# Decoder block pair on one core: stick-breaking q and k, gates and gated projections computed feature-major

## The chip, the cores and the metric

One core of one Trainium2 chip. The metric is the device time of one launch in microseconds, the median of several executions. Everything is float32 outside; the large products run in three matmuls of a rounded float32 type (fp32r), as told below.

## The reference, cut to what matters

Two transformer layers in a row over 256 tokens with 2048 features. The change lies in the second one, whose core is:

```python
proj = h @ w_in
c_q, c_kv, k_pe, q_sb, k_sb, v_sb, gl_a, gl_b = jnp.split(proj, [...], axis=-1)
...
y_a = _mla_attention(...)            # 8 heads
# stick-breaking attention, 8 heads of 128, on q_sb, k_sb, v_sb
z = einsum('bhqd,bhkd->bhqk', qb, k) * 128 ** -0.5
log_beta = log_sigmoid(z)
log_one_minus = where(mask, log_sigmoid(-z), 0.0)
tail = cumsum(log_one_minus, axis=3, reverse=True) - log_one_minus
a = where(mask, exp(log_beta + tail), 0.0)
y_b = einsum('bhqk,bhkd->bhqd', a, v)
...
merged = sigmoid(gl_a) * (y_a @ w_proj_mla) + sigmoid(gl_b) * (y_b @ w_proj_sb)
x = x + gt1 * (merged @ w_out)
```

q_sb, k_sb and v_sb have 1024 features each, gl_a and gl_b 2048 each.

## The kernel before, in words

**Chunks.** All weights are read once, in chunks of 256 input features by 512 output features (512 KB). SP fetches each into `raw`, a ring of four (`sp_chunk`, L301). ScalarE rounds it to `hi` (`act_chunk`, L309), VectorE forms the rest `lo = raw - hi` (`dve_chunk`, L315), and TensorE multiplies (`pe_chunk`, L317 to L333). The operand (activations) is also held in two parts, `op_hi` and `op_lo`, with features in the partitions and 256 tokens in the columns. In `pe_chunk` the operand is the stationary side (128 features x 128 tokens, loaded as weights) and the chunk's 512 output features stream past it; for two token tiles and two feature tiles of the contraction there are three matmuls each: hi with hi (L328), lo with hi (L329), hi with lo (L330), 12 in all. The result has tokens in the partitions. It collects in one of two pairs of PSUM banks (`acc`), and an eviction frees the pair. `chunk_used` counts chunks that TensorE has finished, `lo_ready` those that it may take; ScalarE may round into a ring place when the chunk four earlier is used.

**The order of the second layer** is written out by hand over a chunk number G, the same on each engine (`sp_second`, `act_second`, `dve_second`, `pe_second`). Each engine walks G and does its part of chunk G, then the side steps hung on that G. The stages that the change touches, in order: G 17 to 24 first half of stick q; then latent up-projections; `in2b`, 40 chunks: second half of q, k (two blocks), v (two blocks), eight chunks a block; `in2c`, 64 chunks: the eight gate blocks, sigmoid at the eviction; `pp`, 32 chunks: y_a and y_b times their projections, four chunks a block; `out2`, 32 chunks. ENDS gives the chunk at which block n of the 36 is complete; its eviction is hung on the third G after that (`act_read2`, L1847 to L1849).

**Stick attention** runs beside the gates in four groups of two heads, 16 chunks a group (`stick_at`). Within a group, at the step given (an engine's own step: ScalarE and VectorE run up to three chunks ahead of TensorE): 2 ScalarE copies q, k, v of two heads from `proj` to `s_in` (L1927); 3 TensorE transposes q and k, eight 128x128 blocks (L2284); 6 ScalarE and VectorE copy them to `s_qk`, q scaled (L1930, L2097); 5 TensorE scores (L2295, L2296); 8 ScalarE and VectorE log-sigmoids, TensorE the tail sums; 11 and 12 exponential and mask, TensorE times v (L1836 to L1838); 14 the eviction to `y_b`.

**Gated projections.** VectorE multiplies each finished pp block into its gate (L2195) and adds the two halves (L2199), counted in `gated`. The sum is in `proj` with tokens in the partitions; to be the operand of the output projection it must have features in the partitions. `pe_merged` transposes it (L2318, four 128x128 blocks per pair of feature tiles, eight pairs), ScalarE evicts to `stage` (L494), and VectorE rounds to `op_hi` (L508) and subtracts to `op_lo` (L509), counted in `op_ready`.

**Other lines named:** L1131 matmuls of 128 columns in the first layer's recurrence; L2326 to L2328 the key product (`pe_key_product`, G 16): there the weights, 64 columns wide, are the stationary side, and op_hi and op_lo with 256 tokens stream past, 16 contraction tiles by three matmuls into one place.

Of the kernel before, what the change touches and what calls it, by code (L numbers as in the profile page):

```python
# [24 lines left out]
P = 128  # L25
# [80 lines left out]
def build_program(nc, a, out):  # L106
    V, A, T = nc.vector, nc.scalar, nc.tensor
    with ExitStack() as ctx:
# [101 lines left out]
        with ExitStack() as use:  # L210
# [10 lines left out]
            with ExitStack() as inner:  # L221
                s_in = sb("s_in", [P, TT, 3, GW], stack=inner)
                s_qk = sb("s_qk", [P, GH_HEADS, 2 * S], stack=inner)
                s_l = sb("s_l", [P, GH_HEADS, TRI], stack=inner)
                s_n = sb("s_n", [P, GH_HEADS, TRI], stack=inner)
# [66 lines left out]
        for name, n in (("h1", 8), ("rec", 4), ("ffn1", 8), ("h2", 8), ("merged", 8), ("ffn2", 8)):  # L292
            OG[name] = g
            g += n
# [1074 lines left out]
        def sp_gu(sp, n, w):  # L1369
# [4 lines left out]
            def pair(i, with_ada):  # L1374
                for c, (m, k) in enumerate(pair_order(i)):
                    sp_chunk(sp, CH[f"gu{n}"] + c, i, 16, src(i, m, k))
                    if with_ada:
                        if n == 2 and not later(i) and c == 3:
                            sp.wait_ge(op_ready, OG["merged"] + 8)
                        ada_at(i, c)  # L1380
# [364 lines left out]

        def in2_src(G):
# [68 lines left out]
        sk = {n: sem("stick_" + n) for n in ("in", "tr", "q", "k", "z", "l", "n", "b", "tail", "w", "e", "a", "o", "op")}  # L1815
# [6 lines left out]
        gated = sem("gated")  # L1822
# [24 lines left out]
        def act_read2(act, n, dst, func):  # L1847
            done2(act, n)
            A.activation(dst, acc[:, bank2(n)], func).then_inc(acc_free[bank2(n)], 1)  # L1849
# [68 lines left out]
        def act_stick(act, g, at):  # L1918
            if at == 2:
                if g == 0:  # L1920
                    act.wait_ge(ml["o"], GROUPS)
                    act.wait_ge(acc_free[bank2(15)], freed2(15))
                else:
                    act.wait_ge(sk["o"], g)
                src = proj[:, :, SB0:FREE0].rearrange("p t (d n) -> p t d n", d=3)[:, :, :, g * GW:(g + 1) * GW]
# [19 lines left out]
        def act_second(act):  # L1945
            h2 = lambda g: act_operand(act, OG["h2"], 8, lambda m: mod[:, m:m + 1], lambda m: ada[:, m:m + 1], only=[g])
            merged = lambda g: act_operand(act, OG["merged"], 8, None, only=[g])
            for G in range(G_END):
# [5 lines left out]
                if n is not None:  # L1954
# [8 lines left out]
                    elif n == 3:  # L1963
                        act_read2(act, n, proj[:, :, SB0:SB0 + NB], ACT.Copy)
# [4 lines left out]
                    elif n < 16:  # L1969
                        act_read2(act, n, proj[:, :, SB0 + (n - 10) * NB:SB0 + (n - 9) * NB], ACT.Copy)  # L1970
                    elif n < 24:
                        act_read2(act, n, gate_cols(n - 16), ACT.Sigmoid)
# [23 lines left out]
                for g in range(GROUPS):  # L1996
                    if 2 <= G - mla_at(g) <= 8:
                        act_mla(act, g, G - mla_at(g))
                    if 2 <= G - stick_at(g) <= 14:
# [94 lines left out]
        def dve_stick(dve, cd, g, at):  # L2094
            if at == 6:
                dve.wait_ge(sk["q"], g + 1)
                V.tensor_copy(s_qk[:, :, S:2 * S], tp[:, :, S:2 * S]).then_inc(sk["k"], 1)  # L2097
# [15 lines left out]
        def dve_second(dve, cd, out_readout):  # L2113
            merged = lambda g: dve_operand(dve, cd, OG["merged"], 8, 0, only=[g])
            after = dve_second_steps(dve, "in2", xw2)
            for G in range(G_END):
# [57 lines left out]
                for g in range(GROUPS):  # L2174
                    if 3 <= G - mla_at(g) <= 10:
                        dve_mla(dve, cd, g, G - mla_at(g))
                    if 6 <= G - stick_at(g) <= 12:
# [96 lines left out]
        def pe_stick(pe, g, at):  # L2274
            if at == 3:
                pe.wait_ge(sk["in"], g * 2 + 2)
                if g:
                    pe.wait_ge(sk["w"], g)
                else:
                    pe.wait_ge(ml["pt"], GROUPS)  # L2280
                for h in range(GH_HEADS):
                    for j in range(2):
                        for t in range(TT):
                            ins = T.transpose(tp[:, h, (2 * j + t) * P:(2 * j + t + 1) * P], s_in[:, t, j, h * P:(h + 1) * P], ident)  # L2284
                ins.then_inc(sk["tr"], 1)
            if at == 5:
                pe.wait_ge(sk["q"], g + 1)
                pe.wait_ge(sk["k"], g + 1)
# [4 lines left out]
                for h in range(GH_HEADS):  # L2293
                    q, kk = s_qk[:, h, 0:S], s_qk[:, h, S:2 * S]
# [9 lines left out]
            if at == 11:  # L2304
                pe.wait_ge(sk["a"], g + 1)
                for h in range(GH_HEADS):
                    ins = causal_product(aux[:, h], [s_in[:, t, 2, h * P:(h + 1) * P] for t in range(TT)], s_b[:, h])
                ins.then_inc(sk["o"], 1)

        def pe_merged(pe, g):  # L2310
            j = g // 2
            pe.wait_ge(gated, j + 1)
            Gm = OG["merged"] + g
            pe.wait_ge(stage_ready, CK * (Gm - 1))
            for kk in range(CK):
                for t in range(TT):
                    col = (CK * (g % 2) + kk) * P
                    ins = T.transpose(tp[:, Gm % 2, kk * S + t * P:kk * S + (t + 1) * P], gate_cols(j)[:, t, col:col + P], ident)  # L2318
            ins.then_inc(tp_ready, 1)
# [11 lines left out]
        def pe_second(pe, h2):  # L2331
            n = 0
            for G in range(G_END):
# [5 lines left out]
                if G == 16:  # L2339
                    pe_key_product(pe, c, B2 + n)  # L2340
                elif G < G_UP:
                    k = G % 8 if G < 16 else G - 17
# [30 lines left out]
                for g in range(GROUPS):  # L2373
                    if 0 <= G - mla_at(g) <= 7:
                        pe_mla(pe, g, G - mla_at(g))
                    if 3 <= G - stick_at(g) <= 11:
# [3 lines left out]
                for j in (0, 1):  # L2380
                    if G - (G_PP + 9 + 8 * j) in (0, 1):
                        pe_merged(pe, 2 * j + G - (G_PP + 9 + 8 * j))
                if G in (G_OUT - 2, G_OUT - 1):
                    pe_merged(pe, 4 + G - (G_OUT - 2))
                if G in (G_OUT + 1, G_OUT + 2):
                    pe_merged(pe, 6 + G - (G_OUT + 1))
# [156 lines left out]
```

## Time and profile before

| what | value |
|---|---|
| median of 3 runs | 2608.74 us (2608.72 to 2609.54) |
| span of the profiled execution, first to last instruction | 2606.9 us |
| what lies around the span, by the median | 1.8 us |
| instructions | 33516 |
| TensorE matmuls, busy | 11881, 2587.1 us |
| weight loads, busy | 11881, 2145.5 us |
| VectorE, ScalarE busy | 1825.4 us, 1414.8 us |
| read from memory | 578.55 MB, 223 GB/s over the span |

The profiled execution's own total isn't reported apart from its span, so the median stands for it. PE is TensorE's matmuls, PEld its weight loads, DVE VectorE, ACT ScalarE. Rows of matmuls overlap: each row runs from its issue to the modelled end of its drain, so the pace is read from the distances of the starts, not from the durations. A product of plain float32 shows as two matmuls.

### The profile page before, as it was taken

To read this page: it belongs to the slowest core of one execution; us is meant where nothing else is said; L and a number is where in the kernel's file an instruction comes from. 1 tells how busy PE (TensorE), PEld (TensorE's weight loads), DVE (VectorE), ACT (ScalarE), POOL (GpSimd) and SP (SyncE) were. 2 spreads that over 40 slices of the span, in tenths; PEclk is the share of its full clock that TensorE was granted. 3 is DMA by queue.
4 is the path that set the end of the run, shared out by engine and by line. 5 is a ranking of instruction groups with operands and counts; after the bars stand their busy time and mean duration, and the time that the engine had idled before them with its cause. 6 is when DMAs were issued, how large, how long until landed. Compare 5 with 4: busy or idle time off the path is not lost.

```text
span 2606.9 us, 33516 instructions
## 1 busy us (share of the span) xinstructions
PE 2587.1 (99%) x11881; PEld 2145.5 (82%) x11881; DVE 1825.4 (70%) x2168; ACT 1414.8 (54%) x1861; POOL 14.6 (1%) x28
## 2 busy tenths in 40 slices
PE   9999999999999999999999999999999999999999
PEld 7888888878888888888788888888788888888887
DVE  5888888777777878888875545566687654445565
ACT  6555545465656465445566556544465556565443
POOL 1000000000000000000000000000000000000000
PEclk9999999999999999999999999999999999999999
DMA  7765556778888888887665555555578765655554
GB/s 247 253 194 178 170 151 205 268 262 291 283 292 285 291 285 297 283 293 253 199 202 157 167 171 160 184 204 186 183 269 289 254 198 191 195 190 197 192 193 172
DMA packets 302590, 582.20 MB, mean 223 GB/s; under 512 B 20133, under 2 KB 20913, under 8 KB 302097
## 3 DMA queue, kind: packets, MB, share of 16 engines
q1 hardware_dynamic: 301008, 576.26, 66.7%
q0 software_dynamic: 1008, 3.55, 0.4%
q8 instruction: 70, 1.15, 0.2%
q10 hardware_dynamic: 464, 0.93, 0.1%
q14 instruction: 40, 0.32, 0.0%
HBM read 578.55 MB, written 2.11 MB: 223 GB/s over the span
## 4 chain that ended last, share of the span: by engine, by line
PE 95%; DVE 3%; ACT 1%; issue 1%; DMA 0%; ACTq 0%; DVEq 0%
PE acc L328 30%; PE acc L330 30%; PE acc L329 30%; DVE lo L315 1%; PE aux L1131 1%; DVE op_lo L509 0%; PE tp L482 0%; DVE op_hi L508 0%; ACT stage L494 0%; PE tp L1105 0%; PE aux L2258 0%; PE aux L2257 0%; PE tp L542 0%; DMA rows<-attn_norm_w 0%; PE tp L1151 0%
## 5 line engine op out<-in xcount | busy, mean ns | idle before, releaser
L315 DVE TENSOR_TENSOR lo<-raw,hi 128x1024 fp32r<-128x1024 f32 x895 | 1077.2, 1222 | 430.5 <-ACT hi L309 409.6
L309 ACT ACTIVATE hi<-raw 128x1024 fp32r<-128x1024 f32 x895 | 928.3, 1056 | 528.5 <-PE acc L330 368.8
L328 PE MATMUL acc<-hi,op_hi 128*128 128x512 f32 x2752 | 1084.9, 394 | 8.5 <-DVE lo L315 5.9
L330 PE MATMUL acc<-hi,op_lo 128*128 128x512 f32 x2752 | 1072.1, 390 | 0.0
L329 PE MATMUL acc<-lo,op_hi 128*128 128x512 f32 x2752 | 1071.5, 389 | 0.0
L328 PEld LDWEIGHTS acc<-hi,op_hi 128*128 128x128 f32 x2752 | 516.9, 188 | 119.6 <-issue 11.2
L330 PEld LDWEIGHTS acc<-hi,op_lo 128*128 128x128 f32 x2752 | 516.6, 188 | 109.0
L329 PEld LDWEIGHTS acc<-lo,op_hi 128*128 128x128 f32 x2752 | 517.2, 188 | 102.6
L591 DVE SCALAR_TENSOR_TENSOR ada_acc<-ada_ring,cact,ada_acc 128x512 f32<-128x512 f32 x360 | 269.5, 749 | 7.6 <-DVE small L431 0.6
L328 PE MATMUL acc<-hi,f_hi 128*128 128x512 f32 x704 | 274.5, 390 | 0.1
L329 PE MATMUL acc<-lo,f_hi 128*128 128x512 f32 x704 | 273.9, 389 | 0.0
L330 PE MATMUL acc<-hi,f_lo 128*128 128x512 f32 x704 | 273.9, 389 | 0.0
L1408 ACT ACTIVATE hid<-f_g 32x256 f32 (+1 forms) x352 | 146.3, 416 | 66.7 <-DVE f_g L1473 58.7
L1575 ACT ACTIVATE f_hi<-hid 128x512 fp32r<-128x512 f32 x88 | 55.6, 632 | 227.4 <-PE acc L330 227.4
L328 PEld LDWEIGHTS acc<-hi,f_hi 128*128 128x128 f32 x704 | 132.2, 188 | 27.8 <-issue 0.5
L330 PEld LDWEIGHTS acc<-hi,f_lo 128*128 128x128 f32 x704 | 132.2, 188 | 27.4
L329 PEld LDWEIGHTS acc<-lo,f_hi 128*128 128x128 f32 x704 | 132.2, 188 | 27.2
L1595 DVE TENSOR_TENSOR f_lo<-hid,f_hi 128x512 fp32r<-128x512 f32 x88 | 60.8, 691 | 95.3 <-ACT f_hi L1575 94.7
L735 ACT ACTIVATE proj<-acc,small 128x512 f32<-128x512 f32 x32 | 20.3, 685 | 56.0 <-PE acc L330 54.8
L508 DVE CAST op_hi<-stage 128x512 fp32r<-128x512 f32 x41 | 17.4, 425 | 42.4 <-ACT stage L494 42.2
L1849 ACT ACTIVATE proj<-acc 128x1024 f32<-128x1024 f32 x23 | 23.6, 1027 | 22.8 <-PE acc L330 22.6
L1131 PEld LDWEIGHTS aux<-h_qd,h_kd 128*128 128x128 f32 x256 | 33.5, 191 | 2.5
(336 smaller groups left out, 1284.0 us busy)
## 6 DMA issues: line engine op xcount, KB each, us to landing
raw<-w_in SPq DMA_DIRECT2D x257, 512.0 KB, 3.9
ada_ring<-w_ada SPq DMA_DIRECT2D x192, 512.0 KB, 5.3
raw<-w_gate_up SPq DMA_DIRECT2D x176, 512.0 KB, 5.2
raw<-w_ffn_in SPq DMA_DIRECT2D x176, 512.0 KB, 4.4
raw<-w_down SPq DMA_DIRECT2D x88, 512.0 KB, 5.8
raw<-w_ffn_out SPq DMA_DIRECT2D x88, 512.0 KB, 4.3
raw<-w_out SPq DMA_DIRECT2D x64, 512.0 KB, 4.1
raw<-w_proj_mla SPq DMA_DIRECT2D x16, 512.0 KB, 3.9
```

What stands on the lines that cost most here:

```text
L309: A.activation(hi[:, k, :, 0:n], raw[:, k, :, 0:n], ACT.Copy).then_inc(hi_ready, 1)
L315: V.tensor_tensor(lo[:, k, :, 0:n], raw[:, k, :, 0:n], hi[:, k, :, 0:n].bitcast(F32), ALU.subtract).then_inc(lo_ready, 1)
L328: T.matmul(dst, lh, hi[:, k, kk, 0:n], start=first and kk == 0, stop=False)
L329: T.matmul(dst, lh, lo[:, k, kk, 0:n], start=False, stop=False)
L330: mm = T.matmul(dst, ll, hi[:, k, kk, 0:n], start=False, stop=last and kk == CK - 1)
L591: ins = V.scalar_tensor_tensor(out=ada_acc[:], in0=ring[:, j, kk], scalar=cact[:, m:m + 1], in1=ada_acc[:], op0=ALU.mult, op1=ALU.add)
L735: ins = A.activation(proj[:, t, dst0:dst0 + NB], src[:, t], func, scale=r0[:, t:t + 1])
L1131: ins = T.matmul(aux[:, s % 2, x4 * P:(x4 + 1) * P], kd[:, x4 * P:(x4 + 1) * P], qd[:, y4 * P:(y4 + 1) * P], start=True, stop=True)
L1408: A.activation(dst, src, ACT.Copy).then_inc(f["ev"], 1)
L1575: A.activation(f_hi[:, j % 2], hid[:, 2 * kc:2 * kc + 2, :], ACT.Copy).then_inc(f["sp"], 1)
L1595: V.tensor_tensor(f_lo[:, j % 2], hid[:, 2 * kc:2 * kc + 2, :], f_hi[:, j % 2].bitcast(F32), ALU.subtract).then_inc(lo_done, 1)
L1849: A.activation(dst, acc[:, bank2(n)], func).then_inc(acc_free[bank2(n)], 1)
```

## The change

Stick q, stick k, the gates and the projections of y_a and y_b are computed with the weights as the stationary side (`pe_turned`): for each of four feature tiles of 128 and two contraction tiles, 128x128 of `hi` or `lo` are loaded and 256 tokens of op_hi or op_lo stream past, three matmuls each, 24 a chunk. The result has features in the partitions. The four feature tiles of a block lie in the pair of banks as (bank f // 2, half f % 2). Stick v, the latents, the up-projections and the output projection stay as they were. `s_in`, `s_qk`, the transposes of q and k, `pe_merged` and its stages are gone; v is read from `proj` directly; q's scale is applied when its block is evicted; the merged sum is copied by ScalarE from `proj` to `op_hi`, and VectorE subtracts.

```diff
+        def pe_turned(pe, c, into, kt, first, last, right=(op_hi, op_lo)):
+            k = c % RING
+            pe.wait_ge(lo_ready, c + 1)
+            for f in range(NB // P):
+                for kk in range(CK):
+                    rh, rl = (o[:, kt + kk] for o in right)
+                    dst = into[:, f // 2, f % 2 * S:(f % 2 + 1) * S]
+                    wh, wl = (r[:, k, kk, f * P:(f + 1) * P] for r in (hi, lo))
+                    T.matmul(dst, wh, rh, start=first and kk == 0 and f % 2 == 0, stop=False)
+                    T.matmul(dst, wh, rl, start=False, stop=False)
+                    mm = T.matmul(dst, wl, rh, start=False, stop=last and kk == CK - 1 and f % 2 == 1)
+            mm.then_inc(chunk_used, 1)
...
+        def turned_head(which, head):
+            c0 = SB0 + which * DH + head // 4 * NB + head % 2 * S
+            return proj[:, head % 4 // 2, c0:c0 + S]
+
+        def merged_pair(g):
+            return gate_cols(g // 2)[:, g % 2]
...
+        def act_merged(act, g):
+            act.wait_ge(gated, g // 2 + 1)
+            if g >= 4:
+                act.wait_ge(chunk_used, C2 + G_OUT - 7 + g)
+            A.activation(op_hi[:, CK * g:CK * g + CK].rearrange("p k s -> p (k s)"), merged_pair(g), ACT.Copy).then_inc(merged_hi, 1)
...
         def act_stick(act, g, at):
-            if at == 2:
...
-                for t in range(TT):
-                    A.activation(s_in[:, t], src[:, t], ACT.Copy).then_inc(sk["in"], 1)
-            if at == 6:
-                act.wait_ge(sk["tr"], g + 1)
-                A.activation(s_qk[:, :, 0:S], tp[:, :, 0:S], ACT.Copy, scale=float(P) ** -0.5).then_inc(sk["q"], 1)
...
                     elif n < 24:
+                        if n == 23:
+                            act.wait_ge(sk["o"], GROUPS)
                         act_read2(act, n, gate_cols(n - 16), ACT.Sigmoid)
...
+            def merged(g):
+                dve.wait_ge(merged_hi, g + 1)
+                h, l = (o[:, CK * g:CK * g + CK].rearrange("p k s -> p (k s)") for o in (op_hi, op_lo))
+                V.tensor_tensor(l, merged_pair(g), h.bitcast(F32), ALU.subtract).then_inc(merged_ready, 1)
...
         def pe_stick(pe, g, at):
-            if at == 3:
...
-                            ins = T.transpose(tp[:, h, (2 * j + t) * P:(2 * j + t + 1) * P], s_in[:, t, j, h * P:(h + 1) * P], ident)
...
                 for h in range(GH_HEADS):
-                    q, kk = s_qk[:, h, 0:S], s_qk[:, h, S:2 * S]
+                    q, kk = (turned_head(j, GH_HEADS * g + h) for j in range(2))
...
             if at == 8:
                 pe.wait_ge(sk["n"], g + 1)
+                if g:
+                    pe.wait_ge(sk["w"], g)
+                else:
+                    pe.wait_ge(ml["pt"], GROUPS)
...
-                    ins = causal_product(aux[:, h], [s_in[:, t, 2, h * P:(h + 1) * P] for t in range(TT)], s_b[:, h])
+                    c0 = SB0 + 2 * DH + (GH_HEADS * g + h) * P
+                    ins = causal_product(aux[:, h], [proj[:, t, c0:c0 + P] for t in range(TT)], s_b[:, h])
...
-        def pe_merged(pe, g):
...
@@ pe_second
+                elif 16 < G < G_UP:
+                    pe_turned(pe, c, into, CK * (G - 17), G == 17, G == G_UP - 1)
...
-                    pe_chunk(pe, c, 0, 4, into, CK * k, k == 0, k == 7)
+                    if G_SB + 24 <= G < G_GATE:
+                        pe_chunk(pe, c, 0, 4, into, CK * k, k == 0, k == 7)
+                    else:
+                        pe_turned(pe, c, into, CK * k, k == 0, k == 7)
...
-                        pe_chunk(pe, c, 0, 4, into, CK * (k % 2), k == 0, k == 3, left=(ya_hi[k // 2], ya_lo[k // 2]))
+                        pe_turned(pe, c, into, CK * (k % 2), k == 0, k == 3, right=(ya_hi[k // 2], ya_lo[k // 2]))
...
-                        pe_chunk(pe, c, 0, 4, into, HEADS + CK * k, k == 0, k == 3)
+                        pe_turned(pe, c, into, HEADS + CK * k, k == 0, k == 3)
...
-                        pe.wait_ge(op_ready, OG["merged"] + k + 1)
+                        pe.wait_ge(merged_ready, k + 1)
```

## Rows read from the trace of the kernel before

**Rows 1.** The page: span, busy time by engine, TensorE's granted clock by slice.
```profile
span 2606.9 us, 33516 instructions
...
PE 2587.1 (99%) x11881; PEld 2145.5 (82%) x11881; DVE 1825.4 (70%) x2168; ACT 1414.8 (54%) x1861; POOL 14.6 (1%) x28
...
PEclk9999999999999999999999999999999999999999
```

**Rows 2.** The page: the chain that ended last, by engine.
```profile
PE 95%; DVE 3%; ACT 1%; issue 1%; DMA 0%; ACTq 0%; DVEq 0%
```

**Rows 3.** Waits of TensorE, 1299 to 1800 us: total us, times, longest.
```profile
PE acc L328 <- DVE lo L315: 0.4, 1, 0.4
```

**Rows 4.** Windows: length, busy PE, PEld, DVE, ACT, POOL (counts), clock, DMA, GB/s.
```profile
1298.92:1320.50 21.58, 21.58 (x104) 17.54 (x103) 20.86 (x27) 11.31 (x21) 0.00 (x0) 1.00 0.60 195
1361.10:1441.60 80.50, 80.14 (x404) 67.66 (x403) 45.78 (x57) 50.38 (x96) 0.00 (x0) 1.00 0.54 169
1496.30:1692.20 195.90, 195.90 (x948) 164.92 (x947) 99.01 (x90) 119.67 (x122) 0.00 (x0) 1.00 0.56 172
1692.20:1782.20 90.00, 90.00 (x411) 74.38 (x409) 59.65 (x62) 37.72 (x43) 1.07 (x2) 1.00 0.57 199
```

**Rows 5.** Timeline of PE (start us, us): 12 matmuls of 512, then 48 of 256.
```profile
1289.91 0.39 PE L328 MATMUL acc<-hi,op_hi 128*128 128x512 f32 x1
...
1292.40 0.39 PE L330 MATMUL acc<-hi,op_lo 128*128 128x512 f32 x1
1292.63 0.28 PE L2326 MATMUL acc<-op_hi,hi 128*64 128x256 f32 x1
...
1297.96 0.28 PE L2328 MATMUL acc<-op_lo,hi 128*64 128x256 f32 x1
```

**Rows 6.** Timeline of PEld around a block of eight 128-wide matmuls, first layer.
```profile
121.23 0.86 PEld L1131 LDWEIGHTS aux<-h_qd,h_kd 128*128 128x128 f32 x7
122.01 0.19 PEld L328 LDWEIGHTS acc<-hi,op_hi 128*128 128x128 f32 x1
122.12 0.19 PEld L329 LDWEIGHTS acc<-lo,op_hi 128*128 128x128 f32 x1
```

**Rows 7.** Timeline of PE around the first block of eight stick transposes.
```profile
1507.06 0.39 PE L330 MATMUL acc<-hi,op_lo 128*128 128x512 f32 x1
1507.29 1.03 PE L2284 MATMUL tp<-plain,s_in 128*128 128x128 f32 x8
...
1508.40 0.40 PE L329 MATMUL acc<-lo,op_hi 128*128 128x512 f32 x1
```

**Rows 8.** Timeline of PE around the first block of four merged transposes.
```profile
1719.31 0.39 PE L330 MATMUL acc<-hi,ya_lo 128*128 128x512 f32 x1
1719.54 0.60 PE L2318 MATMUL tp<-plain,proj 128*128 128x128 f32 x4
...
1720.21 0.39 PE L329 MATMUL acc<-lo,ya_hi 128*128 128x512 f32 x1
```

**Rows 9.** Groups by line, 1490 to 1805 us: count, busy us, mean ns, idle before.
```profile
L494 ACT ACTIVATE stage<-tp 128x256 f32<-128x256 f32 x16 | 5.3, 382 | 16.8 <-PE tp L2318 16.8
L2318 PE MATMUL tp<-plain,proj 128*128 128x128 f32 x32 | 4.8, 272 | 0.0
L2284 PE MATMUL tp<-plain,s_in 128*128 128x128 f32 x32 | 4.1, 272 | 0.0
L508 DVE CAST op_hi<-stage 128x512 fp32r<-128x512 f32 x8 | 3.4, 425 | 7.3 <-ACT stage L494 7.3
```

**Rows 10.** Timeline of PE: score products in plain float32, 256 and 128 wide.
```profile
1513.62 0.59 PE L2295 MATMUL aux<-s_qk 128*128 128x256 f32 x2
...
1514.05 0.38 PE L2296 MATMUL aux<-s_qk 128*128 128x128 f32 x2
...
1514.27 0.60 PE L2295 MATMUL aux<-s_qk 128*128 128x256 f32 x2
```

**Rows 11.** Timeline of DVE at the start of the output projection.
```profile
1783.38 1.22 DVE L2199 TENSOR_TENSOR proj<-proj 128x1024 f32<-128x1024 f32 x1
```

More of the change, by code:

```diff
@@ L291, in build_program @@
         g = 0
-        for name, n in (("h1", 8), ("rec", 4), ("ffn1", 8), ("h2", 8), ("merged", 8), ("ffn2", 8)):
+        for name, n in (("h1", 8), ("rec", 4), ("ffn1", 8), ("h2", 8), ("ffn2", 8)):
             OG[name] = g
@@ L1378, in pair @@
                         if n == 2 and not later(i) and c == 3:
-                            sp.wait_ge(op_ready, OG["merged"] + 8)
+                            sp.wait_ge(merged_ready, 8)
                         ada_at(i, c)
@@ L1812, in done2 @@
             eng.wait_ge(chunk_used, C2 + END_OF[n] + 1)
-        sk = {n: sem("stick_" + n) for n in ("in", "tr", "q", "k", "z", "l", "n", "b", "tail", "w", "e", "a", "o", "op")}
+        sk = {n: sem("stick_" + n) for n in ("z", "l", "n", "b", "tail", "w", "e", "a", "o", "op")}
         lt = {n: sem("latent_" + n) for n in ("sq", "var", "root", "ready", "tr", "ev", "split")}
@@ L1821, in build_program @@
         s_ang = sem("angles")
-        gated = sem("gated")
+        gated, merged_hi, merged_ready = sem("gated"), sem("merged_high"), sem("merged_ready")
         added, tail = sem("added"), sem("last_scaled")
@@ L1844, in latent, with act_read2 @@
             return proj[:, :, j * S:(j + 1) * S]
-        def act_read2(act, n, dst, func):
+        def act_read2(act, n, dst, func, scale=1.0):
             done2(act, n)
-            A.activation(dst, acc[:, bank2(n)], func).then_inc(acc_free[bank2(n)], 1)
+            A.activation(dst, acc[:, bank2(n)], func, scale=scale).then_inc(acc_free[bank2(n)], 1)
+        def act_merged(act, g):
[3 more added lines that the diff above has]
+            A.activation(op_hi[:, CK * g:CK * g + CK].rearrange("p k s -> p (k s)"), merged_pair(g), ACT.Copy).then_inc(merged_hi, 1)
         def act_latent_squares(act, l):
@@ L1946, in act_second @@
             h2 = lambda g: act_operand(act, OG["h2"], 8, lambda m: mod[:, m:m + 1], lambda m: ada[:, m:m + 1], only=[g])
-            merged = lambda g: act_operand(act, OG["merged"], 8, None, only=[g])
+            merged = lambda g: act_merged(act, g)
             for G in range(G_END):
@@ L1963, in act_second @@
                     elif n == 3:
-                        act_read2(act, n, proj[:, :, SB0:SB0 + NB], ACT.Copy)
+                        act_read2(act, n, proj[:, :, SB0:SB0 + NB], ACT.Copy, float(P) ** -0.5)
                     elif n < 11:
@@ L1969, in act_second @@
                     elif n < 16:
-                        act_read2(act, n, proj[:, :, SB0 + (n - 10) * NB:SB0 + (n - 9) * NB], ACT.Copy)
+                        act_read2(act, n, proj[:, :, SB0 + (n - 10) * NB:SB0 + (n - 9) * NB], ACT.Copy,
+                                  float(P) ** -0.5 if n == 11 else 1.0)
                     elif n < 24:
+                        if n == 23:
+                            act.wait_ge(sk["o"], GROUPS)
                         act_read2(act, n, gate_cols(n - 16), ACT.Sigmoid)
@@ L2274, in pe_stick @@
         def pe_stick(pe, g, at):
-            if at == 3:
[L2276 to L2283, printed above, removed]
-                            ins = T.transpose(tp[:, h, (2 * j + t) * P:(2 * j + t + 1) * P], s_in[:, t, j, h * P:(h + 1) * P], ident)
-                ins.then_inc(sk["tr"], 1)
             if at == 5:
-                pe.wait_ge(sk["q"], g + 1)
-                pe.wait_ge(sk["k"], g + 1)
+                if g == 0:
+                    for n in (14, 15):
+                        pe.wait_ge(acc_free[bank2(n)], freed2(n))
                 if g:
@@ L2306, in pe_stick @@
                 for h in range(GH_HEADS):
-                    ins = causal_product(aux[:, h], [s_in[:, t, 2, h * P:(h + 1) * P] for t in range(TT)], s_b[:, h])
+                    c0 = SB0 + 2 * DH + (GH_HEADS * g + h) * P
+                    ins = causal_product(aux[:, h], [proj[:, t, c0:c0 + P] for t in range(TT)], s_b[:, h])
                 ins.then_inc(sk["o"], 1)
-        def pe_merged(pe, g):
[L2311 to L2319, printed above, removed]
         def pe_key_product(pe, c, b):
@@ L2340, in pe_second @@
                     pe_key_product(pe, c, B2 + n)
+                elif 16 < G < G_UP:
+                    pe_turned(pe, c, into, CK * (G - 17), G == 17, G == G_UP - 1)
                 elif G < G_UP:
-                    k = G % 8 if G < 16 else G - 17
+                    k = G % 8
                     pe_chunk(pe, c, 0, 4, into, CK * k, k == 0, k == 7, late=OG["h2"] + 1 if G == 0 else None)
```

25 lines of the change are left out of this document (3 added, 22 removed).

## Prediction, made before the changed kernel ran

> **What bounds the kernel now.** I read the page first. TensorE is busy for 2587.1 of 2606.9 us at a granted clock of nine tenths or more in every slice, so at the upper of its two levels, 2.4 GHz [rows 1]. The chain that ended last is 95% TensorE [rows 2]. The reader should not conclude from a busy engine alone that it is the bound, since matmul rows overlap; so I asked what TensorE waited for over the stretch that the change touches: one wait of 0.4 us in 501 us [rows 3]. The windows, cut at the edges of the four touched stages (first half of stick q; second half and k; gates; gated projections), say the same: TensorE fills them, at clock 1.00, but for 0.36 us in the second [rows 4]. VectorE and ScalarE have slack in all but the first (VectorE 20.86 of 21.58 us in the q block), and there TensorE still doesn't wait. Hence the price of any edit is the time it adds to or takes from the row of matmul starts, and what it does on the other engines costs nothing while they keep ahead.
>
> **Base of the sum.** The profiled execution spans 2606.9 us; the runs have a median of 2608.7 (2608.7 to 2609.5). What lies around the span is 1.8 us, which I add back at the end.
>
> **What is taken off TensorE.** Transposes of stick q and k: 32 of them, in four blocks of 8, and transposes of the merged rows: 32, in eight blocks of 4 [rows 9]. A block's price is the delay of the matmuls behind it, not its busy time. For the block of 8: from the start of the matmul ahead of it (1507.06) to the start of the second matmul behind it (1508.40) are 1.34 us, where two plain steps of 0.227 would stand; 0.89 us are the block's [rows 7]. For the block of 4: 1719.31 to 1720.21 is 0.90, less 0.454, so 0.45 us [rows 8]. Sum: 4 x 0.89 + 8 x 0.45 = 7.1 us.
>
> **What is changed on TensorE.** 128 chunks are turned: 8 (q, first half), 24 (q second half and k), 64 (gates), 32 (gated projections). A chunk was 12 matmuls with 512 moving columns and becomes 24 with 256; both stream 6144 columns, but the number of loads of 128 weight columns doubles. The 512-wide step: 11 of them between 1289.91 and 1292.40, so 0.2264 us; I use 0.227. The only matmuls of this kernel that stream 256 columns of the rounded type are the key product's: 47 steps from 1292.63 to 1297.96, 0.1134 us each [rows 5]. By that, a turned chunk takes 24 x 0.1134 = 2.72 us and an unturned one 12 x 0.227 = 2.72: nothing gained or lost. These 48 also all add into one and the same place, so the loop order of the change (six matmuls in a row into one feature tile) is covered by the row.
>
> But the key product loads 64 weight columns, not 128. Does a load of 128 fit behind 256 streamed columns? The nearest row is the HGRN block of 128-wide matmuls, where loads come as fast as they can: 8 steps from 121.23 to 122.12, 0.111 us each [rows 6]. 0.111 is under 0.113, so the load just hides. The slack falls from 0.227 - 0.111 = 0.116 us in the present chunk to 0.002 us. That is the weak joint of the sum. I take 0.1134, the row nearest in moving shape, and bound it: below, 0.1134 too (no row streams these columns faster); above, 0.120, for a reason given under the second rival. One step's uncertainty counts 128 x 24 = 3072 times: 1 ns is 3.1 us, and 2.3 ns eat the whole gain of 7.1.
>
> **What moves on other engines.** Gone: eight ScalarE copies of s_in, four ScalarE and four VectorE copies of s_qk, the 16 evictions of the merged transposes (382 ns) and 8 VectorE casts (425 ns) [rows 9]; in place of the last two stand 8 ScalarE copies of 512 columns straight from proj. Nobody on TensorE waited for these, so their saving is nothing, and the new ones cost nothing while TensorE stays the bound. The scale moves into an eviction that exists. The score products read proj in place of s_qk, same shapes, no change. No DMA is added or removed, and SP's queue keeps its order; the one wait that moves there (before the second FFN's first modulation columns) counts the same eight operands, now ready sooner.
>
> **Waits added.** ScalarE's merged copy waits for the gated sum, with the next weight roundings queued behind it on ScalarE. The last such sum ends at 1783.38 + 1.22 = 1784.6 [rows 11]; the operand is wanted by chunk 6 of the output projection, which begins at 1782.2 (the end of the last window) + 6 x 2.72 = 1798.5. Twelve us of room; the rounding for chunk 4 is wanted some 8 us after. The copies for the upper half wait for TensorE to have left op_hi, at a point where the ring of four already held ScalarE to the same chunk. The tail product waits for s_b's subtraction, a wait that the transposes used to carry earlier; there are six chunks between. The eighth gate's eviction waits for the last stick product, emitted seven chunks earlier. If this cover went (a chunk late by one copy), some 1 us per place would be added.
>
> **Sum.** 2606.9 - 7.1 + 0 = 2599.8 in the span, + 1.8 = 2601.6 us. About 0.2% (5 us) is what a measurement of this kernel can tell from no change, and the forecast clears that by 2 us only.
>
> **Rivals.** First, **a fixed cost per matmul.** In full-precision products a 256-wide step is 0.215 us (1513.62 to 1514.05, two passes of one product) and a 128-wide one 0.110 (1514.05 to 1514.27, two again) [rows 10]: two halves cost 5 ns more than the whole. If that held for the rounded type, 1536 more matmuls cost 7.7 us: 2609.3, no change. Against it: 2 x 0.1134 is 0.2268, no more than the 512-wide step [rows 5]. It would also look like this if the load's 0.111 carried a few ns that the row of 128-wide matmuls hides. The Trainium skill (TensorE: Matmul & The Clock Gate, Back-to-back issue gap) gives a warm gap of N/2.4 + 2.5 ns; by it 12 x 215.8 becomes 24 x 109.2, 31 ns more a chunk, 4.0 us in all, and the result would be an estimated 2605.6, no measurable change. The trace does not agree with its size at 512 (227 here), nor shows its fixed part in this type.
>
> Second, ending slower, **weight loads that slow the stream.** The 512-wide step is 0.227 where 512 columns at 2.4 GHz are 0.2133: 13.7 ns over. The key product's is 0.1134 where 256 are 0.1067: 6.7 ns over. I read this as a cost in proportion to columns streamed. But both have one loaded column to four streamed, so it may as well be in proportion to columns loaded: 13.7 ns for each load of 128. Then a turned step is 0.1067 + 0.0137 = 0.120 us, a chunk 2.89 against 2.72, and 3072 x 6.7 ns = 20.6 us are added: 2622.2. It decides from 115.7 ns a step on. Nothing in the trace separates the two; for mine speaks that full-precision matmuls with the same loads have only 2 ns over 0.2133 [rows 10], against it that they stream at half the rate and leave room. The Trainium skill (same page, What happens when you issue a matmul) says of the two read ports that loading the next weights doesn't steal bandwidth from the running matmul; by that this rival is void and the time 2601.6, but no row here shows it.
>
> Third, that the change does less than it says, the removed blocks being hidden anyway: excluded by [rows 3], as TensorE has no idle time for them to hide in. A late merged operand or a late rounding is the rest.
>
> **How the numbers follow.** Forecast 0.50; fixed cost or a load a few ns too long 0.20; loads slowing the stream 0.25; anything else 0.05. Its own range is 2600 to 2604. With both unknown-price rivals of opposite sign so near, the range goes from 2600 to 2623. Faster by over 0.2%: most of the first case (0.46) and a little of the second, 0.48. Within: 0.22. Slower: the second rival and the rest, 0.30.
>
> **What would show it.** Right: matmuls of the turned line with 256 columns starting every 0.113 us, 2.72 us a chunk, the lines of the transposes gone, the gates' 64 chunks ending some 3.5 us sooner after the same start, no wait on TensorE. A step of 0.116 to 0.117 says the first rival; 0.120, with weight loads that fill the window, the second. Steps of 0.113 with the time unchanged would mean that a wait has come up, and the waits list would name ScalarE's merged copy or VectorE's lo.

## The result and the profile after

The changed kernel takes 2620.24 us (2619.98 to 2621.06), the one before 2608.8: ratio 1.0045, 95% interval 1.003 to 1.0059. It is slower by 11.4 us. The span went from 2606.9 to 2618.4 us, and what lies around it stayed at 1.8. The forecast was 2601.6 in a range of 2600 to 2623, and the second rival's price 2622.2.

The page of the changed kernel, the lines that answer to [rows 1] and [rows 2]:

```profile
span 2618.4 us, 36413 instructions
...
PE 2598.6 (99%) x13353; PEld 2219.3 (85%) x13353; DVE 1819.9 (70%) x2156; ACT 1406.8 (54%) x1841; POOL 14.6 (1%) x28
...
PEld 7888888878888888887889899998788888888887
...
PEclk9999999999999999999999999999999999999999
...
PE 96%; DVE 2%; ACT 0%; issue 0%; DMA 0%; ACTq 0%; DVEq 0%
```

There are 1472 more matmuls (1536 for the turned chunks, less 64 transposes). The clock is the same in every slice, and the chain is even more TensorE's. The row of weight loads (PEld) changed most: it turned to nines in five slices between 1375 and 1767 us, where the turned stages lie.

The windows of the changed kernel, cut at the same chunks as [rows 4], and the output projection as a fifth (columns: length, busy PE, PEld, DVE, ACT, POOL with counts, clock, DMA share, GB/s):

```profile
1298.74:1320.50 21.76, 21.76 (x184) 21.56 (x183) 20.95 (x27) 11.08 (x20) 0.00 (x0) 1.00 0.59 190
1361.94:1445.38 83.44, 83.44 (x693) 83.03 (x692) 45.80 (x57) 50.62 (x96) 0.00 (x0) 1.00 0.53 164
1500.07:1702.15 202.08, 202.08 (x1683) 201.65 (x1682) 96.52 (x86) 110.88 (x109) 0.00 (x0) 1.00 0.56 167
1702.15:1794.40 92.25, 92.25 (x771) 92.24 (x770) 57.75 (x56) 39.30 (x40) 1.07 (x2) 1.00 0.61 194
1794.40:1888.60 94.20, 93.54 (x407) 74.92 (x405) 54.93 (x60) 43.95 (x57) 0.00 (x0) 1.00 0.57 180
```

Read them by length. Stick q's second half and k: 83.4 for 80.5 us before. Gates: 202.1 for 195.9, although four blocks of transposes are gone from them. Gated projections: 92.3 for 90.0. The first window is cut short of its stage's end in both kernels; from its start to the first latent matmul are 24.8 for 23.8 us. The output projection is shorter, for two of the eight merged blocks stood there; the same stage of the kernel before, cut to its own edges, read:

```profile
1782.15:1877.41 95.26, 94.61 (x415) 75.81 (x414) 56.11 (x64) 44.44 (x61) 0.00 (x0) 1.00 0.52 177
```

So the five stages add 1.0, 2.9, 6.2, 2.3 and -1.1 us, which is 11.3 of the 11.5 us that the span grew by.

In the gated projections the loads are busy for all of the window (92.24 of 92.25), where they were busy for 83% before (74.38 of 90.00).

The step itself, timeline of TensorE in a gated-projection chunk (start us, duration us), 22 steps between first and last:

```profile
1751.56 0.28 PE L342 MATMUL acc<-ya_hi,hi 128*128 128x256 f32 x1
1751.68 0.28 PE L343 MATMUL acc<-ya_lo,hi 128*128 128x256 f32 x1
1751.80 0.28 PE L344 MATMUL acc<-ya_hi,lo 128*128 128x256 f32 x1
...
1754.20 0.28 PE L343 MATMUL acc<-ya_lo,hi 128*128 128x256 f32 x1
```

(1754.20 - 1751.56) / 22 = 0.120 us. It is so in every one of the 128 turned chunks: their means are 0.1193 to 0.1200, leaving out the longer steps (0.2 us and more) that stand right behind a matmul of another kind. TensorE's list of waits for 1299 to 1815 us, which had one entry of 0.4 us [rows 3], is empty: nothing is waited for, the steps are longer.

### The profile page after: what moved, and what is told of

Read it like the earlier page. It is cut to its first block, busy times and chain, and to the rows that moved or that the text cites. A ratio compares the mean times of both kernels' runs of the same rounds, so it can differ in the third digit from the quotient of the medians.

```text
span 2618.4 us, 36413 instructions
## 1 busy us (share of the span) xinstructions
PE 2598.6 (99%) x13353; PEld 2219.3 (85%) x13353; DVE 1819.9 (70%) x2156; ACT 1406.8 (54%) x1841; POOL 14.6 (1%) x28
## 4 chain that ended last, share of the span: by engine, by line
PE 96%; DVE 2%; ACT 0%; issue 0%; DMA 0%; ACTq 0%; DVEq 0%
PE acc L326 26%; PE acc L327 26%; PE acc L328 26%; PE acc L342 5%; PE acc L343 5%; PE acc L344 5%; PE aux L1143 1%; DVE lo L313 1%; DVE op_lo L521 0%; PE tp L494 0%; DVE op_hi L520 0%; ACT stage L506 0%; PE tp L1117 0%; PE aux L2274 0%; PE aux L2275 0%
## 5 line engine op out<-in xcount | busy, mean ns | idle before, releaser
L326 PE MATMUL acc<-hi,op_hi 128*128 128x512 f32 x2304 | 907.0, 394 | 8.2 <-DVE lo L313 5.6
L328 PE MATMUL acc<-hi,op_lo 128*128 128x512 f32 x2304 | 897.5, 390 | 0.0
L327 PE MATMUL acc<-lo,op_hi 128*128 128x512 f32 x2304 | 897.1, 389 | 0.0
L327 PEld LDWEIGHTS acc<-lo,op_hi 128*128 128x128 f32 x2304 | 432.9, 188 | 86.0
L342 PE MATMUL acc<-op_hi,hi 128*128 128x256 f32 x896 | 255.8, 286 | 0.0
L344 PE MATMUL acc<-op_hi,lo 128*128 128x256 f32 x896 | 253.5, 283 | 0.0
L343 PE MATMUL acc<-op_lo,hi 128*128 128x256 f32 x896 | 253.5, 283 | 0.0
L342 PEld LDWEIGHTS acc<-op_hi,hi 128*128 128x128 f32 x896 | 171.9, 192 | 0.2
L343 PEld LDWEIGHTS acc<-op_lo,hi 128*128 128x128 f32 x896 | 171.9, 192 | 0.1
L344 PEld LDWEIGHTS acc<-op_hi,lo 128*128 128x128 f32 x896 | 171.8, 192 | 0.0
```

Of the source, the lines that this page charges most:

```text
L342: T.matmul(dst, wh, rh, start=first and kk == 0 and f % 2 == 0, stop=False)
L343: T.matmul(dst, wh, rl, start=False, stop=False)
L344: mm = T.matmul(dst, wl, rh, start=False, stop=last and kk == CK - 1 and f % 2 == 1)
```

## Experiments

**Four theories** stood at the start. A: a weight load takes time from the stream (the second rival). B: the load of 128 columns has a floor of its own, 0.120 us, under such a stream. C and D: other engines' traffic, or adding six times in a row into one place. Where a run leaves something out or computes something else, its expectation says what.

### The two halves of the change by themselves

`e2_wide_steps`: the changed kernel, its turned chunks stepped as before.

```diff
-            for f in range(NB // P):
+            for t in range(TT):
                 for kk in range(CK):
...
+                    T.matmul(dst, lh, hi[:, k, kk], start=first and kk == 0, stop=False)
+                    T.matmul(dst, lh, lo[:, k, kk], start=False, stop=False)
+                    mm = T.matmul(dst, ll, hi[:, k, kk], start=False, stop=last and kk == CK - 1)
```

> The changed kernel with the 128 turned chunks stepped as before (12 matmuls of 512 streamed columns, operand stationary), all else as changed. These chunks then deliver their products in the other orientation, so the results of stick attention and of the merged sum are not the reference's; the work of every engine is otherwise that of the changed kernel. It isolates what the removal of the transposes is worth. My forecast's term: 2608.8 - 7.1 = 2601.7 us. By the difference of after and before and a step of 0.120 (3072 x 6.6 ns = 20.3 added, 11.4 measured) the removal is worth 8.9: 2599.9. If a wait or another engine had cost part of the 11.4, this would stay above 2603.

Measured: 2601.25 us (2600.50 to 2601.48), ratio 0.997, interval 0.9959 to 0.9982. Against 2608.64 for the kernel before, measured beside it, that is 7.4 us less; the forecast's term was 7.1. TensorE's list of waits for 1299 to 1815 us has one entry, as before:

```profile
PE acc L341 <- DVE lo L313: 0.4, 1, 0.4
```

`e5_turned_steps`: the kernel before, with `pe_turned` called for the same 128 chunks.

```diff
...
-                    pe_chunk(pe, c, 0, 4, into, CK * k, k == 0, k == 7)
+                    if G_SB + 24 <= G < G_GATE:
+                        pe_chunk(pe, c, 0, 4, into, CK * k, k == 0, k == 7)
+                    else:
+                        pe_turned(pe, c, into, CK * k, k == 0, k == 7)
...
```

> The kernel before with the same 128 chunks multiplied in turned steps and nothing else changed (the transposes stay, and as the orientation of these blocks doesn't match what reads them, the results of the second layer's attention and gates are not the reference's). It isolates the cost of the steps. With 3072 x (0.1200 - 0.1134) = 20.3: 2629.1 us. If the cost per step depended on how they stand between blocks of transposes (I suspect so, as after a block the 512-wide steps ran at 0.231 to 0.236 for a while), less: about 2627. If the steps cost what was forecast, 2608.8.

Measured: 2627.49 us (2627.22 to 2628.14), ratio 1.0071, interval 1.0055 to 1.0088: 18.85 us more. 18.85 - 7.4 = 11.45, and 11.4 is what the change measured. The parts add up: all of the change but its steps gives 7.4 us back, the steps cost 18.85, and no new wait or other engine adds anything that the time shows. The steps cost 18.85 / 3072 = 6.1 ns each on balance. The wait of 0.4 us for VectorE, absent from this run's list and present in the run with wide steps, is the part of it that the slower pace covers.

### Order of the loops

`e3_kk_outer`:

```diff
-            for f in range(NB // P):
-                for kk in range(CK):
+            for kk in range(CK):
+                for f in range(NB // P):
```

> The changed kernel with the contraction tile as the outer loop of a turned chunk and the feature tile as the inner: three matmuls in a row into one place instead of six. If the 0.120 us step comes from loads, as theories A and B say, the order doesn't matter: 2620.2 us, step 0.120. If repeated adding into the same PSUM place slowed it (theory D), shorter: fewer repeats, below 2618.

Measured: 2620.27 us (2619.67 to 2620.95), ratio 1.0043, interval 1.0026 to 1.0060. The step is 0.120 again, so the loop order of the change isn't the cause. Three additions in a row into one place are left in this run; what takes D out altogether are two series below, one that alternates two places and still needs 0.120, and one that adds 24 times in a row into one place with shorter loads and needs 0.1133.

### Stick alone, gates and projections alone

Each is the change with the other part left as in the kernel before; both compute the reference.

```diff
...
-                    if G_SB + 24 <= G < G_GATE:
+                    if G_SB + 24 <= G:
                         pe_chunk(pe, c, 0, 4, into, CK * k, k == 0, k == 7)
...
```

> Only stick q and k turned (32 chunks), gates, gated projections and merged transposes as in the kernel before. Turned steps cost 32 x 24 x 6.1 ns = 4.7 us by the run with turned steps alone; the four blocks of eight transposes give back 4 x 0.89 = 3.6: 2608.6 + 1.1 = 2609.7 us, no measurable change. If the 32 chunks cost less than their share (the first eight stand in a stretch where VectorE is 97% busy and may hide part), 2608 or below.

Measured: 2609.05 us (2608.63 to 2609.75) against 2608.67, ratio 1.0002, interval 0.9992 to 1.0012.

```diff
...
-                    pe_chunk(pe, c, 0, 4, into, CK * k, k == 0, k == 7)
+                    if G < G_GATE:
+                        pe_chunk(pe, c, 0, 4, into, CK * k, k == 0, k == 7)
+                    else:
+                        pe_turned(pe, c, into, CK * k, k == 0, k == 7)
...
```

> The complement of the run with stick q and k alone turned: gates and gated projections turned, the merged sum copied and subtracted without transposes, stick attention as in the kernel before. If the parts add up (after +11.5, stick part +0.4): 2608.7 + 11.1 = 2619.8 us. By single prices: 96 x 24 x 6.1 ns = 14.1 added, 8 x 0.45 = 3.6 taken off: 2619.2. If the new waits of ScalarE's merged copy cost something that the full change hides elsewhere, above 2621, and TensorE's waits would name them.

Measured: 2619.88 us (2619.69 to 2620.42) against 2609.24, ratio 1.0041, interval 1.0026 to 1.0056. So stick's turning pays for itself and no more: 32 chunks against four blocks of eight transposes, eight chunks a block. The 96 gate and projection chunks stand against eight blocks of half that size, twelve chunks a block, and that is where 10.6 of the 11.4 us are lost.

### The step measured by itself

`e1_shapes` appends series of 24 rounded matmuls behind the last product of the kernel before, when the other engines are nearly idle:

```diff
+            def series(width, cols, dst, n=24):
+                for j in range(n):
+                    T.matmul(dst[0:width, 0:cols], op_hi[:, j % KT, 0:width], wide[j % 2][:, 0:cols], start=j == 0, stop=j == n - 1)
+            series(128, 512, tp[:, 0])
...
```

> The kernel before, with ten series of 24 rounded matmuls each appended behind its last product, into a PSUM bank that nothing else uses by then, at (loaded columns, streamed columns). The changed kernel's step was 0.120 us where 0.1134 was forecast. Theory A, a load takes time from the stream: step = (streamed + loaded/4) / 2.4 GHz. Theory B, the stream takes 17/16 of its columns whatever is loaded, and a load of 128 has a floor of 0.120 us under such a stream: step = the larger of the two. (128,512): A 0.2267, B 0.2267. (64,512): A 0.2200, B 0.2267. (32,512): A 0.2167, B 0.2267. (128,384): A 0.1733, B 0.1700. (128,256): both 0.1200. (96,256): A 0.1167, B 0.1133. (64,256): both 0.1133. (32,256): A 0.1100, B 0.1133. (128,128) and (64,128): A 0.0667 and 0.0600 unless the load itself is the floor (some 0.111 and 0.056), B 0.120 and 0.060. If other engines' traffic were behind the 0.120 (theory C), these series, which run when the others have almost nothing to do, would show less than 0.120 at (128,256). The time as a whole is longer by the series, some 30 us.

Windows of that run on TensorE, each cut from the first start of a series to its last, so a window is 23 steps (the counts take in matmuls that reach into the window). In order: (loaded, streamed) = (32,512), (128,384), (128,256), (64,256), (32,256), (128,128).

```profile
2612.50:2617.83 5.33, 5.33 (x24) 1.00 0.00 0
2618.06:2622.08 4.02, 4.02 (x25) 1.00 0.00 0
2622.25:2625.00 2.75, 2.75 (x25) 1.00 0.00 0
2627.90:2630.50 2.60, 2.60 (x25) 1.00 0.00 0
2630.62:2633.22 2.60, 2.60 (x25) 1.00 0.03 6
2633.34:2635.86 2.52, 2.52 (x26) 1.00 0.00 0
```

The steps: 0.2317, 0.1748, 0.1196, 0.1130, 0.1130 and 0.1096 us (the edges are rounded to 0.01; by the starts in nanoseconds the two 0.1130 are 0.1133). The series that aren't shown: (128,512) 0.2267, (64,512) 0.2300, (96,256) 0.1160 as a mix of steps of 0.112 and 0.121, (64,128) 0.0599. C is out: with no transfers and idle engines, (128,256) is still 0.120. A wants 0.110 at (32,256) and 0.2167 at (32,512) and gets neither, so the 17/16 of the stream is there without the load. B as a plain floor wants 0.170 at (128,384) and 0.120 at (128,128), and gets 0.175 and 0.110. What stays is plain: 256 streamed columns need 0.113 behind a short load; a load of 128 needs 0.110 where only 128 columns stream (last row; with 64 loaded the same stream needs 0.060, so it is the load that sets this pace); and together they need 0.120.

`e9_more_shapes` put a rule to the test that I had drawn from these series.

```diff
+            series(80, 256, tp[:, 0])
+            series(112, 256, tp[:, 1])
...
+            for j in range(24):
+                T.matmul(tp[:, j % 2, 0:(512, 256)[j % 2]], op_hi[:, j % KT, 0:P], wide[j % 2][:, 0:(512, 256)[j % 2]], start=j < 2, stop=j >= 22)
```

> The kernel before with further series of rounded matmuls behind its last product, to test a rule found from the first ten series: step = the larger of 17/16 of the streamed columns and streamed plus a quarter of the loaded columns, at 2.4 GHz. (80 loaded, 256 streamed) 0.1150; (112,256) 0.1183; (128,320) 0.1467 against 0.1417 if only 17/16 counted; (128,448) 0.2000; (64,384) 0.1700; (96,384) 0.1700; (128,512) 0.2267; (128,192) 0.0933 unless a load's own floor of 0.110 to 0.120 holds. The last series alternates 512 and 256 streamed columns, 128 loaded: the rule says 0.3467 a pair, the run with one load for two products had 0.3513 a pair in the kernel; 0.351 here too would mean that the sequence matters, 0.347 that the kernel's other traffic made the difference.

The rule fell: (112,256) needed 0.1133 where it said 0.1183, (64,384) 0.173 for 0.170, (96,384) 0.175 for 0.170, (128,448) 0.203 for 0.200, (128,512) 0.228 for 0.2267, and the alternating pair 0.352 for 0.347. (128,320) and (80,256) came near, 0.1475 for 0.1467 and 0.1140 for 0.1150; (128,192) stands at 0.111, a load's own pace. The window of (112,256), first start to last, 23 steps:

```profile
2604.87:2607.47 2.60, 2.60 (x25) 1.00 0.38 147
```

`e6_types` changed what is read.

```diff
+            halved, half = sem("halved"), proj[:, 1, 6000:7024].bitcast(mybir.dt.bfloat16)
...
+            series(w, lambda j: r(j, 256), [tp[:, 0, 0:256], tp[:, 1, 0:256]])
+            series(lambda j: op_hi[:, 0, 0:P], lambda j: op_hi[:, 1], [tp[:, 0, 0:256]])
...
+            series(lambda j: ob[:, 128 * (j % 8):128 * (j % 8) + 128], lambda j: hb[:, 0:512], [tp[:, 0]])
```

> The kernel before, with seven series appended behind its last product. Rounded float32, (128 loaded, 256 streamed), results into two banks in turn: 0.120 if the place of the result doesn't matter. The same with one and the same block of weights each time: 0.120 if every matmul loads anyway; 0.113 if a repeated block costs less. Plain float32, (128,256): 0.215 as in the score products. Operands of two bytes (bfloat16): if the reads of four-byte operands by load and stream get in each other's way, halving the bytes takes it off: (128,512) 0.215 to 0.216 and (128,256) 0.108 to 0.110, (64,256) the same. If the cost has nothing to do with bytes: 0.2267, 0.120 and 0.1133. (128,128) of two bytes shows the floor of a load: some 0.056 to 0.111.

Windows on TensorE of 23 steps each; in order: one block of weights each time, rounded float32 (128,256); bfloat16 (128,512), (128,256), (128,128). The three of bfloat16 run from the second start of a series to the first of the next.

```profile
2604.16:2606.92 2.76, 2.76 (x25) 1.00 0.33 123
2612.44:2617.40 4.96, 4.96 (x23) 1.00 0.00 0
2617.51:2620.02 2.51, 2.51 (x25) 1.00 0.00 0
2620.08:2621.45 1.37, 1.37 (x25) 1.00 0.00 0
```

A repeated block of weights is loaded anew each time (24 loads in the trace, 0.120 a step), and two result banks in turn change nothing (0.1197). With two-byte operands (128,512) needs 0.2157 and (128,256) 0.109: no 17/16, and no extra for the load. At (128,128) the steps are 0.056; the window's last, 0.149, is the step to the next series. Plain float32 at (128,256), in the same run, needs 0.2159 a matmul, 2.6 ns over 256 columns at half of 2.4 GHz, with four bytes an element and the same loads. So 17/16 and the extra for the load were seen in the rounded type only, and four bytes alone don't make them. What does stays open: in bfloat16 the load's own time falls too (0.056 at (128,128), for 0.110), so this run doesn't tell bytes from a load that is nearly as long as its stream. The Trainium skill (TensorE: Matmul & The Clock Gate, Back-to-back issue gap) has N/2.4 + 2.5 ns, 215.8 and 109.2: the two-byte series agree, the rounded type doesn't, at any width tried.

### Fewer loads, shorter loads, in the kernel

`e4_one_load` joins the two products on one weight block.

```diff
-                    T.matmul(dst, wh, rh, start=first and kk == 0 and f % 2 == 0, stop=False)
-                    T.matmul(dst, wh, rl, start=False, stop=False)
+                    pair = op_both[:, :, kt + kk] if right[0] is op_hi else right[0][:, kt:kt + 2]
+                    T.matmul(into[:, f // 2].rearrange("p (a s) -> p a s", a=2), wh, pair,
+                             start=first and kk == 0 and f % 2 == 0, stop=False)
                     mm = T.matmul(dst, wl, rh, start=False, stop=last and kk == CK - 1 and f % 2 == 1)
```

> The changed kernel with a turned chunk's two products on the same weights joined: one load of 128 columns of hi, then op_hi and op_lo stream as one matmul of 512 columns (for y_a, two contraction tiles of ya_hi stand in for the pair), and lo with op_hi stays 256 wide. The wide matmul writes the whole bank, so the sums are not the reference's (what belongs to one feature tile falls on two); the streamed columns stay 6144 a chunk, the loads fall from 24 to 16. If the step is streamed columns plus a quarter of the loaded ones, at 2.4 GHz: a chunk is 8 x 0.120 + 8 x 0.2267 = 2.773 us in place of 2.88, 128 x 0.107 = 13.7 us less than the changed kernel: 2606.5. If the turned orientation cost something apart from its loads (which operand streams, where it is written), it would stay above 2610.

Measured: 2609.50 us (2608.53 to 2609.86), ratio 1.0002, interval 0.9992 to 1.0012. Eight loads fewer a chunk are worth 10.7 us of the 13.7 expected. A pair takes 0.3487 us in the mean, leaving out the long steps behind other matmuls, where the rule said 0.3467; it is in the wide step, 0.2325 after a 256-wide one, not 0.227. Over 1024 pairs that is 2 of the missing 3 us.

`e10_112_columns` and `e11_64_columns` only shorten the loads (and with them the number of partitions that the result fills); the edit shown is that of the first, the second has 64 in place of 112.

```diff
-                    dst = into[:, f // 2, f % 2 * S:(f % 2 + 1) * S]
-                    wh, wl = (r[:, k, kk, f * P:(f + 1) * P] for r in (hi, lo))
+                    dst = into[0:112, f // 2, f % 2 * S:(f % 2 + 1) * S]
+                    wh, wl = (r[:, k, kk, f * P:f * P + 112] for r in (hi, lo))
```

> The changed kernel with each load of a turned chunk cut from 128 to 112 weight columns; the last 16 of every 128 features of stick q, k, gates and projections are left out (old values stand there), so the results are not the reference's. The same 3072 matmuls with the same 256 streamed columns and the same instructions; only the loads are shorter. In the series behind the kernel, 112 loaded columns gave 0.1133 us and 128 gave 0.1200. If it is the load's length against the stream that costs the 0.120, the step is 0.1133 and the time that of wide steps, 2601.3 us. If it is anything else of the turned chunk (twice the instructions, the operand's place, the order of results), it stays near 2620.

Measured: 2606.28 us (2605.85 to 2606.91), ratio 0.9991, interval 0.9981 to 1.0. The same instructions, the same streamed columns, and 14 us less than the changed kernel: the length of the load (128 columns) is what makes the steps dear. That it fell 5 us short of the expected 2601.3 goes with a second level of the step, told below. The mean step is 0.1153, and 3072 x (0.11993 - 0.1153) = 14.2 is the whole difference. It isn't the number of partitions written, for bfloat16 fills all 128 at 0.109.

> As the run with 112 loaded columns, but with 64 of every 128 (half of the features of stick q, k, gates and projections left out). With 112 the steps fell from 0.1199 us to a mix of 0.113 to 0.114 and 0.117 to 0.119, mean 0.1153. With 64 the step should be the key product's 0.1134 throughout, and the time 2620.2 - 3072 x 6.5 ns = 2600.3 us; the forecast's own term for the removed transposes then stands by itself. If a mix stays, 2603 to 2606: then the two levels are not a matter of the load's length alone.

Measured: 2604.99 us (2604.49 to 2605.52), ratio 0.9985, interval 0.9975 to 0.9994, against an expected 2600.3. The trace shows why. Timeline of TensorE, the first and last matmul (23 steps apart) of a chunk before and a chunk after one small transpose:

```profile
1703.99 0.28 PE L342 MATMUL acc<-op_hi,hi 128*64 128x256 f32 x1
...
1706.60 0.28 PE L344 MATMUL acc<-op_hi,lo 128*64 128x256 f32 x1
...
1709.43 0.27 PE L1555 MATMUL aux<-plain,ada 128*16 128x128 f32 x1
...
1712.42 0.28 PE L342 MATMUL acc<-ya_hi,hi 128*64 128x256 f32 x1
...
1715.18 0.28 PE L344 MATMUL acc<-ya_hi,lo 128*64 128x256 f32 x1
```

2.61 / 23 = 0.1133 before it, 2.76 / 23 = 0.1200 after, and the 24 chunks that follow the transpose all keep 0.1200, whichever operand they read; the 104 ahead of it have 0.1133 to 0.1143 (long steps behind other matmuls left out). The run with 112 columns has two levels as well, 0.1133 and 0.1178, held over up to 36 chunks and changed only where other matmuls stand between. So with short loads there is a fast and a slow level; with 128 columns only 0.120 was seen to last, in 128 chunks and three series. The slow level with 64 columns is as slow as with 128, so a short load makes the fast level possible and doesn't secure it. 24 chunks x 24 steps x 6.7 ns = 3.9 us are most of the 4.7 that this run missed its expectation by.

## Why the prediction was wrong, step by step

**What bounds the kernel: right.** TensorE is the bound before and after, without a wait, and each part's price is what it does to the row of starts. That the parts add up to 11.45 agrees with it.

**The removed transposes: right.** 7.1 us forecast (its own terms add up to 7.16), 7.4 measured by themselves. Little of it could be mis-sized, as it was read as the delay of the matmuls behind a block.

**The turned steps: this step failed.** "By that, a turned chunk takes 24 x 0.1134 = 2.72 us ... nothing gained or lost." It takes 24 x 0.120 = 2.88. The mis-sized term is the step of 256 streamed columns with 128 loaded. I took it from the key product, nearest in streamed shape, and checked the load apart, from a block where loads come every 0.111 us [rows 6]. Both figures came back in the series, 0.113 and 0.110, the second with some luck: the block of [rows 6] is of plain float32 (eight matmul rows for four products), whose 128 streamed columns need 0.110 by themselves [rows 10], so that row alone didn't show a load's own pace. The conclusion that the longer of the two sets the pace was wrong, for the two rows were each taken without the other. The section called this the weak joint, with a slack of 2 ns, and still gave it half the chance. The measured 2620.24 lies inside the range of 2600 to 2623 only because that range was stretched to the second rival's price.

**The second rival: right in what happens, right in size by luck.** Loads slow the stream, 0.120 us a step, a price of 2622.2 where 2620.2 was measured. Its formula, 13.7 ns for each load of 128, is refuted: (32,256) is no shorter than (64,256), and (32,512) is longer than (128,512). The sentence of the Trainium skill that I set beside it (TensorE: Matmul & The Clock Gate, What happens when you issue a matmul: loading the next tile's weights doesn't steal read bandwidth from the running matmul) can't be read as "a load costs no time" for rounded float32: 0.1133 becomes 0.120. The series of bfloat16 and of plain float32 agree with that reading (0.109, and 0.2159 at half rate). Whether it is read bandwidth that runs short, no run shows.

**The first rival: not it.** A fixed cost per matmul would show with 64 or 112 loaded columns too, and the same 3072 matmuls ran at 0.1133 for most chunks of one and many of the other.

**The waits: right.** ScalarE's merged copy that waits for the last gated sum starts at 1797.12 and is done by 1797.8; VectorE's part of the same operand is done by 1799.4, and the operand is wanted at 1794.4 + 6 x 2.72 = 1810.7. TensorE's list of waits is empty. What moved on ScalarE and VectorE (8.0 and 5.5 us less busy, by the page) was worth nothing.

**The balance** of 18.85 against 3072 x 6.6 ns = 20.3 is partly the covered 0.4 us wait. The rest, about 1 us, I put down to wide steps running at 0.231 to 0.236 for a while after each block of plain float32, which turned steps don't. The trace of the kernel before bears out the size: in the touched stages 1452 wide steps behind another wide one are 0.96 us longer in all than 1452 x 0.22667. It was not tried by a run.

## What to carry to other kernels

Turning a product so that its result needs no transpose isn't free when the tokens are fewer than the features: the streamed side shrinks from 512 to 256, and the weights are loaded twice as often. When loads and streamed columns are each near the pace, don't take the longer of two rows that were measured apart; look for a row with both, or count such a step as unknown. Here the break-even was about eight turned chunks for each block of eight transposes saved. The Trainium skill (Trainium Kernel Development and Optimization, Best Practices) has the distance to the roofline judged by MFU (the share of peak arithmetic) and by the busy share of LDWEIGHTS, not by that of the matmuls. The windows of the gated projections agree as far as they go: the loads went from 83% to 100%, with the matmuls at 100% in both. No variant that computes the reference beat the kernel before: stick alone equals it, the rest loses.

## What the runs showed of the hardware that I had not expected

- With 256 streamed columns behind a short load, and with 512 behind a load of 128, a rounded-float32 matmul took 17/16 of its columns at 2.4 GHz (0.1133 and 0.2267 us); a bfloat16 one 0.109 and 0.2157.
- In rounded float32 a load of 128 columns (0.110 where only 128 stream) and a stream of 256 (0.113 behind 32 or 64 loaded) make 0.120 together; in bfloat16 they make 0.109, where the load is shorter too. Plain float32 at (128,256) takes 0.2159.
- The pace has levels. With 64 or 112 loaded columns and 256 streamed it stays at 0.1133 over many chunks, or at 0.1200 (64) and 0.1178 (112), and goes from one to the other where a differently shaped matmul intervenes. With 512 streamed, shorter loads brought nothing: one series each gave 0.2300 with 64 loaded and 0.2317 with 32, two with 128 gave 0.2267 and 0.2284. What sets the level stays open; I tried no run that chooses it.
